# Four of the sixteen up-projection units of each MLP computed in seven products instead of eight blocks

## What is computed

```python
def sq_relu_mlp(h, w_up, w_down):
    return jnp.square(jax.nn.relu(h @ w_up)) @ w_down

f = sq_relu_mlp(rmsnorm_2(x, g[2]), w_up, w_down)
x = x + rmsnorm_2(f, g[3])
gate = jax.nn.sigmoid(rmsnorm_2(x, g[4]) @ w_ple_gate[i])
e = (p[i] @ w_ple_proj[i]) * gate
x = x + rmsnorm_2(e, g[5])
```

## Time and profile before

| | us |
|---|---|
| median of 3 runs | 1715.15 (1714.98 to 1716.29) |
| the profiled execution's own time | 1714.86 |
| its span, first to last instruction | 1713.1 |
| PE busy | 1693.0 (99% of the span) |
| PEld busy | 1449.8 (85%) |
| DVE busy | 1198.9 (70%) |
| ACT busy | 918.6 (54%) |
| POOL busy | 169.8 (10%) |

### The profile page before, as it was taken

How to read it: one execution, slowest core, us unless ns; L and a number is a source line. 1 busy time by engine, 2 the same in 40 slices (tenths; PEclk the granted TensorE clock), 3 DMA queues, 4 the chain that set the end, 5 groups by cost and what they waited for, 6 DMA issues and landing times.

```text
span 1713.1 us, 24293 instructions
## 1 busy us (share of the span) xinstructions
PE 1693.0 (99%) x9087; PEld 1449.8 (85%) x9087; DVE 1198.9 (70%) x1848; ACT 918.6 (54%) x1545; POOL 169.8 (10%) x147
## 2 busy tenths in 40 slices
PE   9999999999999999999999999999999999999998
PEld 7888877888788897789898988878887999898977
DVE  6378877776567777576586976785566848587866
...
GB/s 268 85 74 74 40 74 101 74 50 147 74 112 75 74 75 81 74 74 128 71 147 68 130 74 111 110 56 109 107 86 74 99 123 75 123 76 122 111 74 50
DMA packets 151053, 160.68 MB, mean 94 GB/s; under 512 B 18089, under 2 KB 126150, under 8 KB 150694
## 3 DMA queue, kind: packets, MB, share of 16 engines
...
...
## 4 chain that ended last, share of the span: by engine, by line
PE 95%; DVE 2%; ACT 2%; issue 0%; DVEq 0%; ACTq 0%
PE bank L1053 29%; PE bank L1054 29%; PE bank L1055 29%; PE bank L1402 2%; PE bank L1426 1%; PE bank L1321 1%; PE bank L1310 1%; DVE act_a L2485 0%; PE bank L1696 0%; ACT act_a L1793 0%; DVE work L2516 0%; PE bank L1236 0%; PE bank L1220 0%; PE bank L1345 0%; PE bank L1252 0%
## 5 line engine op out<-in xcount | busy, mean ns | idle before, releaser
L1053 PE MATMUL bank<-act_a,split_weights 128*128 128x512 f32 (+1 forms) x1392 | 547.7, 393 | 6.2 <-DVE act_a L2483 2.0
L1055 PE MATMUL bank<-act_a,split_weights 128*128 128x512 f32 (+1 forms) x1392 | 541.1, 389 | 0.0
L1054 PE MATMUL bank<-act_a,split_weights 128*128 128x512 f32 (+1 forms) x1392 | 540.5, 388 | 0.0
L1053 PEld LDWEIGHTS bank<-act_a,split_weights 128*128 128x128 f32 x1392 | 261.6, 188 | 62.9 <-issue 6.0
L1055 PEld LDWEIGHTS bank<-act_a,split_weights 128*128 128x128 f32 x1392 | 261.3, 188 | 55.4
L1054 PEld LDWEIGHTS bank<-act_a,split_weights 128*128 128x128 f32 x1392 | 261.7, 188 | 50.2 <-issue 0.2
L2425 DVE TENSOR_TENSOR split_weights<-raw_weights,split_weights 128x2048 fp32r<-128x2048 f32 x67 | 154.6, 2307 | 147.9 <-ACT split_weights L1738 134.9
L1738 ACT ACTIVATE split_weights<-raw_weights 128x2048 fp32r<-128x2048 f32 x63 | 120.3, 1909 | 199.3 <-PE bank L1055 199.2
L1053 PE MATMUL bank<-act_b,split_weights 128*128 128x256 f32 (+1 forms) x648 | 207.1, 320 | 0.0
L1055 PE MATMUL bank<-act_b,split_weights 128*128 128x256 f32 (+1 forms) x648 | 206.4, 319 | 0.0
L1054 PE MATMUL bank<-act_b,split_weights 128*128 128x256 f32 (+1 forms) x648 | 206.3, 318 | 0.0
...
## 6 DMA issues: line engine op xcount, KB each, us to landing
raw_weights<-in_w_mlp_up SPq DMA_DIRECT2D x32, 1024.0 KB, 5.4
raw_weights<-in_w_mlp_down SPq DMA_DIRECT2D x32, 1024.0 KB, 4.9
raw_weights<-in_w_in SPq DMA_DIRECT2D x18, 1024.0 KB, 5.2
raw_weights<-in_w_conv_in SPq DMA_DIRECT2D x12, 1024.0 KB, 5.1
...
raw_weights<-in_w_ple_gate SPq DMA_DIRECT2D x8, 1024.0 KB, 4.7
raw_weights<-in_w_out SPq DMA_DIRECT2D x4, 1024.0 KB, 4.9
raw_weights<-in_w_attn_in SPq DMA_DIRECT2D x4, 1024.0 KB, 5.3
```

Source lines behind the costliest of these rows:

```text
L1053: nc.tensor.matmul(dst, w[0], a[0], start=first, stop=False)
L1054: nc.tensor.matmul(dst, w[0], a[1], start=False, stop=False)
L1055: mm = nc.tensor.matmul(dst, w[1], a[0], start=False, stop=last)
```

## The change

**Seven products for four up units of each MLP.** `PRODUCT_UPS` names them: unit 2 of chunk 1, units 0 and 2 of chunk 2, unit 2 of chunk 3. Such a unit runs in a new function `mlp_up_products`: seven products of 4 k-pairs x 3 matmuls of 128 x 256, into four banks. Its weights are summed and split as those of a down unit (steps `G` or `I` for three sums, `F` or `K` for the fourth, `g` or `i` for the split of a product). The results of the products are then mixed in PSUM and SBUF by one ACT copy (`o`) and four DVE additions (`d`, `up_mix`) before relu.

**Sums of the inputs.** The products need sums of blocks of the MLP's input. They are made once per MLP, in chunk 0 during the last two down units, in four rounds k: ACT scales two tiles by the norm's gain (`X`), DVE makes four sums of 128 x 256 (`Q`), ACT writes their high parts, three instructions, and DVE their low parts, three more (both `H`).

**Room for them.** They lie where x, the embedding's projection and p are kept. So ACT issues three DMAs to DRAM as the MLP begins (`keep_outside`, 2, 1 and 1 MB) and three back (`bring_back`, step `B`) in the last chunk.

**Other moves.** Up unit 3 of chunks 1 to 3 goes to banks 4 and 5 of `UP_BANKS`, and its weights are split in two halves (`N6 N7`) ahead of the mixing, where they were split in one piece (`U3`) right after unit 1 had ended. Up unit 1 of chunk 2 is split as `N2 N3` while unit 0 runs.

```diff
+PRODUCT_UPS = ((), (2,), (0, 2), (2,))
...
+UP_BANKS = (((0, 1), (2, 3), (4, 5), (6, 7)), ((0, 1), (2, 3), (6, 7, 0, 1), (4, 5)),
+            ((0, 1, 2, 3), (4, 5), (6, 7, 0, 1), (4, 5)), ((0, 1), (2, 3), (6, 7, 0, 1), (4, 5)))
...
+            def mlp_up_products(layer, name, c, u):
+
+                pl = Place(tab, name, 8 * c + u)
+                number = product_unit_number(layer, c, u)
+                for i in range(PRODUCTS):
+                    if i < PRODUCTS - 1:
+                        pe.wait_ge(prod_split, (PRODUCTS - 1) * number + i + 1)
+                    else:
+                        pe.wait_ge(w_split, pl.u + 1)
...
+                    for kp in range(KT // 2):
+                        three(mlp_bank(name, UP_BANKS[c][u][g])[:, TOKENS[half]], [w[hl][:, kp * P:kp * P + P] for hl in (0, 1)],
+                              [up_operand(UP_OPERAND[i], hl, kp) for hl in (0, 1)], half == kp == 0,
+                              kp == KT // 2 - 1 and (half == 1 or g == 0), prod_done if kp == KT // 2 - 1 else None)
...
+                def x_gain(kp):
+                    if kp:
+                        act.wait_ge(x_sum_ready, x_sum_count(layer, kp - 1, 7, 4))
+                    for h in range(2):
+                        k = kp + h * KT // 2
+                        nc.scalar.activation(sq[:, h, :], wt(X + k), ACT.Copy, scale=col(G_NORM2 + 48 * layer + 16 + k))\
+                            .then_inc(x_sum_hi, 1)
+
+                def x_sums_hi(kp):
+                    act.wait_ge(x_sum_ready, x_sum_count(layer, kp, 7, 4))
+                    both = x_sums[:, kp:KT:KT // 2, :]
+                    nc.scalar.activation(both[:, :, TOKENS[0]], x_first_sums(kp), ACT.Copy).then_inc(x_sum_hi, 1)
+                    for what in ("t3", "t4"):
+                        nc.scalar.activation(x_sum(what, 0, kp), x_sum_made(what, kp), ACT.Copy).then_inc(x_sum_hi, 1)
...
+                def keep_outside():
+                    act.wait_ge(x_ready, n["x"])
+                    nc.scalar.dma_start(x_stash, x_tiles).then_inc(stash_saved, 16)
+                    act.wait_ge(tile_read, tab.extra[name] + 4)
+                    nc.scalar.dma_start(e_stash, e_tiles).then_inc(stash_saved, 16)
+                    nc.scalar.dma_start(p_stash, p_parts).then_inc(stash_saved, 16)
+
+                def bring_back():
+                    act.wait_ge(prod_done, product_done(layer, LAST, PRODUCT_UPS[LAST][-1], PRODUCTS - 1))
+                    act.wait_ge(stash_saved, 16 + 48 * (layer + 1))
+                    nc.scalar.dma_start(x_tiles, x_stash).then_inc(stash_back, 16)
+                    nc.scalar.dma_start(e_tiles, e_stash).then_inc(stash_back, 16)
+                    nc.scalar.dma_start(p_parts, p_stash).then_inc(stash_back, 16)
...
+                def up_mix(c, u, step):
...
+                        dve.wait_ge(prod_done, product_done(layer, c, u, 2))
+                        first = ssum[:, TOKENS[0]][:, None, :].to_broadcast((P, 2, S // 2))
+                        V.tensor_tensor(in_halves(sq[:, 0, :]), in_halves(second[:, :]), first, ALU.add).then_inc(up_mixed, 1)
...
+                def x_sums_made(kp):
+                    dve.wait_ge(x_sum_hi, x_sum_count(layer, kp, 5, 2))
...
+                    V.tensor_tensor(t1, b12, b11, ALU.subtract).then_inc(x_sum_ready, 1)
+                    V.tensor_tensor(t3, b22, b12, ALU.subtract).then_inc(x_sum_ready, 1)
+                    dve.wait_ge(x_sum_ready, x_sum_count(layer, kp, 7, 1))
+                    V.tensor_tensor(t2, b22, t1, ALU.subtract).then_inc(x_sum_ready, 1)
+                    dve.wait_ge(x_sum_ready, x_sum_count(layer, kp, 7, 3))
+                    V.tensor_tensor(t4, b21, t2, ALU.subtract).then_inc(x_sum_ready, 1)
```

The strings of steps at the places that matter (the end of chunk 0 for DVE and ACT, the end of the up part of the last chunk for ACT):

```diff
-DVE, chunk 0:  S2 p14 p15 p16 z2 p17 p18 p19 p20 S3 p21 p22 p23 z3 p24 p25 p26 p27 n0 n1 n2 n3
+DVE, chunk 0:  S2 p14 p15 p16 z2 p17 p18 p19 Q0 p20 H0 S3 p21 p22 Q1 p23 z3 p24 p25 H1 p26 p27 n0 Q2 H2 n1 Q3 H3 n2 n3
-ACT, chunk 0:  ... p18 a3 p19 a4 p20 a5 p21 a6 p22 p23 p24 p25 p26 p27 a7 n0 a8 a9 n1 a10 n2 a11 a12 a13 n3
+ACT, chunk 0:  ... p18 X0 a3 p19 a4 H0 p20 a5 p21 a6 X1 p22 p23 p24 H1 p25 p26 p27 a7 n0 X2 a8 H2 a9 n1 X3 a10 H3 n2 a11 a12 a13 n3
-ACT, chunk 3:  U2 s0 b0 t0 v0 U3 s1 b1 t1 v1 p0 ... p13 k0 c0 c1 c2
+ACT, chunk 3:  g14 g15 s0 b0 t0 g16 v0 g17 s1 b1 g18 t1 g19 v1 g20 o2 N6 N7 p0 ... p13 B0 k0 c0 c1 c2
```

More of the change, by code:

```diff
@@ new lines, in up_bank_read, with x_sum @@
+        def up_bank_read(layer, c, b, before=4):
+            for u in reversed(range(before)):
+                if b in UP_BANKS[c][u]:
+                    return up_read(layer, c, u, UP_BANKS[c][u].index(b))
+            if b < PRODUCTS:
+                return product_read(layer, c - 1, 1, b)
+            if c == 1:
+                return tile_read, tab.tile[tab.first[f"mlp{layer}"] + 8]
+            return up_bank_read(layer, c - 1, b)
+        def x_sum(what, hl, kp):
+            if what == "t4":
+                return head_qk[:, 2 * hl + kp // 2, TOKENS[kp % 2]]
+            home = e_sums[:, kp, :] if what == "t3" else x_sums[:, kp + (KT // 2 if what == "t2" else 0), :]
+            return home[:, TOKENS[hl]]
@@ L655, in up_unit_number @@
             return 4 * MLP_CHUNKS * layer + 4 * c + u
-        def down_unit_number(layer, c, d):
-            return (4 * LAST + 2) * layer + 4 * c + d
-        FREES_NEXT = (21, 23, 25, 27)
-        FREES_LAST = (9, 11, 13)
-        ACT_UP = "U3 s1 b1 t1 v1 p0 p1 p2 p3 s2 b2 t2 v2 p4 p5 p6 p7 s3 b3 p8 t3 p9 v3 p10 p11 p12 p13 "
-        ACT_DOWN = "p14 p15 {a0} p16 {a1} p17 {a2} p18 {a3} p19 {a4} p20 {a5} p21 {a6} p22 p23 p24 p25 p26 p27 "             "{a7} n0 {a8} {a9} n1 {a10} n2 {a11} {a12} {a13} n3"
@@ L672, in hybrid_block_kernel @@
-        DVE_DOWN = ("S2 p14 p15 {a0} p16 {a1} z2 p17 {a2} p18 {a3} p19 {a4} p20 {a5} S3 p21 {a6} p22 p23 z3 "
-                    "p24 p25 p26 p27 n0 {a7} {a8} n1 {a9} {a10} n2 {a11} {a12} n3 {a13}")
-        DVE_NEXT = DVE_DOWN.replace("{", "").replace("}", "")
-        DVE_FIRST = " ".join(step for step in DVE_DOWN.split() if step[0] != "{")
-        DVE_MLP = (DVE_UP + DVE_FIRST, "U2 " + DVE_UP + DVE_NEXT, "U2 " + DVE_UP + DVE_NEXT,
-                   "m0 m1 m2 m3 m4 m5 m6 x0 x1 x2 x3 x4 x5 x6 U2 " + DVE_UP +
+        ACT_PLAIN = "U3 s1 b1 t1 v1 p0 p1 p2 p3 s2 b2 t2 v2 p4 p5 p6 p7 s3 b3 p8 t3 p9 v3 p10 p11 p12 p13 "
@@ new lines, in hybrid_block_kernel @@
+        ACT_THIRD = ("g14 g15 s0 b0 t0 g16 v0 g17 s1 b1 g18 t1 g19 v1 g20 o2 N6 N7 p0 p1 p2 p3 s2 b2 t2 v2 "
+                     "p4 p5 p6 p7 s3 b3 p8 t3 p9 v3 p10 p11 p12 p13 ")
+        ACT_MLP = ("s0 b0 t0 v0 " + ACT_PLAIN + "p14 p15 a0 p16 a1 p17 a2 p18 X0 a3 p19 a4 H0 p20 a5 p21 a6 X1 p22 p23 p24 H1 p25 p26 "
+                   "p27 a7 n0 X2 a8 H2 a9 n1 X3 a10 H3 n2 a11 a12 a13 n3",
+                   ACT_THIRD + "p14 p15 p16 p17 p18 p19 p20 p21 p22 p23 p24 p25 p26 p27 i0 i1 i2 i3",
+                   "i4 i5 i6 o0 N2 N3 " + ACT_THIRD + "p14 p15 p16 p17 p18 p19 p20 p21 p22 p23 p24 p25 p26 p27 n0 n1 n2 n3",
+                   ACT_THIRD + "B0 k0 c0 c1 c2 j0 q0 q1 q2 q3 n0 q4 q5 q6 q7")
@@ new lines, in hybrid_block_kernel @@
+        DVE_PLAIN = ("T0 b0 y0 t0 v0 U3 T1 b1 y1 t1 v1 S0 p0 p1 p2 z0 p3 T2 b2 y2 t2 v2 p4 p5 p6 S1 p7 T3 b3 y3 p8 t3 p9 v3 z1 "
+                     "p10 p11 p12 p13 ")
+        DVE_THIRD = ("g14 g15 T0 b0 y0 t0 g16 v0 g17 F2 T1 b1 g18 y1 t1 g19 v1 g20 N6 N7 d8 d9 d10 S0 p0 d11 p1 p2 z0 p3 "
+                     "T2 b2 y2 t2 v2 p4 p5 p6 S1 p7 T3 b3 y3 p8 t3 p9 v3 z1 p10 p11 p12 p13 ")
+        DVE_DOWN = "S2 p14 p15 a0 p16 a1 z2 p17 a2 p18 a3 p19 a4 p20 a5 S3 p21 a6 p22 p23 z3 p24 p25 p26 p27 "
@@ L678, in hybrid_block_kernel @@
+        DVE_MLP = (DVE_PLAIN + "S2 p14 p15 p16 z2 p17 p18 p19 Q0 p20 H0 S3 p21 p22 Q1 p23 z3 p24 p25 H1 p26 p27 n0 Q2 H2 n1 Q3 H3 n2 n3",
+                   "G2 " + DVE_THIRD + DVE_DOWN + "I0 a7 i0 a8 i1 i2 a9 i3 K0",
+                   "A10 i4 i5 i6 A11 A12 d0 N2 d1 d2 N3 A13 G2 d3 " + DVE_THIRD + DVE_DOWN + "n0 a7 a8 n1 a9 a10 n2 a11 a12 n3 a13",
+                   "m0 m1 m2 m3 m4 m5 m6 x0 x1 x2 x3 x4 x5 x6 G2 " + DVE_THIRD +
                    "e0 l0 c0 l1 l2 l3 c1 l4 l5 e1 l6 c2 l7 j0 n0 f0 f1 f2 f3")
@@ L3197, in mlp @@
                         elif what == "T":
[L3198 removed]
+                            hidden_t13(c, k)
                         elif what == "y":
```

309 lines of the change are left out of this document (222 added, 87 removed).

## The result

| | before | after |
|---|---|---|
| median, us | 1715.07 (1714.58 to 1716.29) | 1729.93 (1728.67 to 1730.92) |
| span of the profiled execution | 1713.1 | 1729.1 |
| granted clock, mean of the span | 0.998 | 0.992 |

The ratio is 1.0085, with a 95% interval from 1.0068 to 1.0103: the changed kernel is slower by 14.9 us. The forecast was 1715.7 us, no measurable difference, with a range up to 1723.

What follows compares the result with a forecast made beforehand. PE was taken as the bound, busy 1693.0 of 1713.1 us. Profiled 1714.86 - 6.9 saved + 7.4 of new waits gave 1715.4, median 1715.7 us (no measurable difference), range 1708.0 to 1723.0.

Steps and rivals of the forecast that it cites:

- The saving: Eight up units in products, each at 10.025 instead of 10.885 us on PE: 0.86 us each, 6.9 us in all.
- Place 1: End of chunk 0: input sums delay the split's second half, so PE starts chunk 1 late by 2.9 us per layer.
- The walk instruction by instruction: ACT and DVE followed from p18 at the end of chunk 0: n0 at 804.4, n1 ready at 811.1 us.
- The sum: Per layer 3.4 us saved against 3.7 us of new waits; over both layers 1715.4 us profiled, median 1715.7.
- Place 2: Split of up unit 3 behind a unit in products, three times a layer: PE waits 0.3 us per layer in all.
- just in time: Unit 3's split takes 9.9 of 10.02 us available; in the last chunk PE waits about 0.2 us.
- Place 3: Last chunk: three DMA issues on ACT before k0 delay the first plain down unit, 0.5 us per layer.
- if they share evenly, it lands after twice its 4.9 us, near 1043, in time: Last chunk: the last unit's weight load shares evenly with the returning transfers, so PE does not wait.
- their rival: Last unit's load waits behind all 4 MB returning: PE waits 9.6 us, 19 in two layers, about 1735 us; chance 0.09.
- the two cases that I had: Last unit's load either waits behind all 4 MB, landing at 1055.4, or shares evenly, landing near 1043.
- a decision point: Last unit's load delays PE only if it lands after 1045.8, 13 us after issue.

Runs made afterwards that it cites:

- e6: The changed kernel with transfers back early, third round of input sums behind both halves of unit 0's split, last round behind unit 1's: 1709.61 us, ratio 0.9966.
- e2: The changed kernel with the third and fourth rounds of input sums behind both halves of chunk 1's first unit split: 1722.04 us, ratio 1.0036.
- e4: The changed kernel with 11 needless matmuls keeping PE busy in the wait before chunk 1, no order changed: 1724.34 us, ratio 1.0057.
- e8: The kernel before with needless DVE sums between n0 and n1, making PE idle for six lengths at the starts of chunks 1 to 3: 1738.78 us.
- e1: The changed kernel with the three returning DMA loads issued some 17 us earlier in the last chunk: 1717.74 us, ratio 1.0014.
- e5: The changed kernel with the DRAM areas laid out so that the six transfers move rows of 1 KB: 1739.02 us, ratio 1.0134.
- e10: The kernel before with the six transfers alone, no new unit in products and no input sums: 1726.20 us, ratio 1.0062.
- e9: The changed kernel with the DRAM areas laid out for rows of 2 KB, like the weight load's packets: 1720.35 us, ratio 1.0029.

## Why the prediction was wrong

**The saving: right.** 10.00 to 10.02 us for each up unit in products, as taken from the earlier trace rows; e6 turns 5.6 of the 6.9 us into time.

**Place 1: right, and to 0.1 us.** 2.9 us of wait per layer were forecast, the trace shows 2.64 us named as a wait, and a down part of chunk 0 that takes 2.8 us more than before. e2 shows it is the order n0, Q2, H2, n1 that makes it. The walk instruction by instruction was worth its length.

**Missed behind place 1: the clock.** The sum priced a wait at its own length. Behind it came 1.75 and 1.5 us at 1.2 GHz. e4 takes just these away (3.0 of 3.25 us), e8 makes such stretches in the kernel before. PE had no such wait in the MLPs before, so the earlier trace rows had only the full clock.

**Place 2: cost next to nothing.** Forecast 0.3 us per layer. In the last chunk the half units ended at 1009.86 and PE began at 1009.92: the "just in time" of the walk held, without the 0.2 us before it. Unit 3 itself took 0.13 us longer than before.

**Place 3: the issues cost nothing in the change.** Forecast 0.5 us per layer. The two down units in products ahead of this place took 0.21 and 0.06 us more than before, and in e1, with no issue in front of k0, 0.13 and 0.46 us more, so that is not the issues' doing. By the Trainium skill (Perfetto Trace Analysis, Per-engine timelines) ACT's sequencer is ready for the next instruction once it has pushed one in the wait queue. The timeline of the change agrees (0.33, 0.46 and 0.45 us beside running work); the three issues at the start of the first MLP (0.36, 0.44 and 0.96 us) brought no wait of PE either. It is no guarantee: 1.10 and 0.69 us in e4, 2.95 and 2.88 us in e5 for rows of 1 KB, and in both runs they held k0, by 0.78 and 4.86 us.

**The step that failed: "if they share evenly, it lands after twice its 4.9 us, near 1043, in time".** With it the transfers had no term in the sum, and their rival a chance of 0.09. The trace shows neither of the two cases that I had. The load's first packets move some 3.7 us after its issue; from then on both queues send about as many packets, and those of the return are up to four times as large, so the load gets a fifth of the bytes until the return is through. It landed at 1048.85, 13.54 us after issue, against a decision point that I had put at 13 us. In the second layer it was 14.0 us. The wait at the last unit was 0.84 and 1.23 us, near the 0.5 and 1.0 us that this point gives, and it stood in no term that this delays the squares, the gate's split and so the norm's sums by 2.9 to 3.2 us more, with half clock behind them. Over both layers that makes 11.5 us in e10 and 13.1 in the change. The rival had the right direction, but its price (the load behind all 4 MB, 19 us) was not what happened. The Trainium skill (DMA: Bandwidth & Descriptors, Queues, rings and completion order) says that a DMA engine takes turns between rows at the granularity of packets. The packet counts of e5, e9 and the change agree with turns one to one, where the profile counts single rows as packets. I had read it as equal bytes, and so as speaking against the rival; equal turns with unequal packets speak for it. The row counts of the transfers (128 rows of 16 and 8 KB) were in the code.

**The sum again.** For the profiled execution it was 15.5 us short: the end of the MLPs 13.1 and the clock behind place 1 3.25 had no term, 0.6 us lay ahead of the first MLP, and the three places together cost about 1.3 us less than their 7.4.

**What stays open.** What decides whether the clock falls behind a wait of 2.4 to 3.2 us: it fell behind 2.36 us (e8), 2.64, 2.92 and 3.22 us (the change), and stayed full behind 2.64 (e5, second layer), 2.85 (e8), 2.91 (e10, first layer) and 3.15 us (e4, second layer). And why the first packets of a load come some 3.7 us after issue beside the return: in the kernel before they came after about 1.3 us, and all of it had landed after 4.9.
